# A two-block transformer on one core: joined attention streams, head norms beside a linear, additions on GpSimd and modulation slabs in unused halves of tiles

## The chip, the cores and the metric

One NeuronCore of one Trainium2 chip. The time is that of one launch of the kernel on the device, in microseconds (us). The profile is one execution of it. Engines: PE is TensorE, DVE is VectorE, ACT is ScalarE, POOL is GpSimd, SP is SyncE, which here only issues DMAs.

## The reference

256 latent tokens and 256 context tokens of width 1024 (fp32) go through two blocks of two layers each. Every layer is modulated by six vectors computed from `c` (for the latent) and `c_ctx` (for the context) by a 1024 x 6144 matrix.

```python
def first_block(...):                       # layers 0 (even) and 1 (odd)
    m_lat = split(silu(c) @ ada_w[l] + ada_b[l], 6); m_ctx = split(silu(c_ctx) @ ada_w[l] + ada_b[l], 6)
    h_lat, h_ctx = modulate(x_lat, m_lat[0], m_lat[1]), modulate(x_ctx, m_ctx[0], m_ctx[1])
    # even: 8 heads of global attention (2 kv heads, rms norm of q and k heads, rope), and
    #       8 heads of neighbourhood attention with a bias; odd: window attention with a sink, rope
    y_lat, y_ctx = even_mixer(...) or odd_mixer(...)
    x = layer_norm(DN_ALPHA * x + m[2] * y)
    x = layer_norm(DN_ALPHA * x + m[5] * conv_ffn(modulate(x, m[3], m[4])))

def token_mixer(...):                       # both layers of the second block
    y_a = conformer_conv(h)                 # glu, depthwise conv of 31 taps, norm, silu, projection
    y_b = diff_finish(softmax(q1 k1) v - lam * softmax(q2 k2) v)      # 8 heads of width 128, rope
    y_c = multiscale_pool(h)                # windows 2, 4, 8, 16, a small matrix per group
    g = sigmoid(h @ w_g + b_gate)
    return (g[..., :D] * y_a + g[..., D:2 * D] * y_b + g[..., 2 * D:] * y_c) @ w_out

def second_block(...):
    x = x + gt1 * rms_norm_2(token_mixer(rms_norm_2(x) * (1 + sc1) + sh1))
    x = x + gt2 * rms_norm_2(swiglu(rms_norm_2(x) * (1 + sc2) + sh2))
```

Layer 0 of a block computes latent and context (512 columns), layer 1 only the latent (256 columns), with the context entering its keys and values. The output is the latent after the second block.

## The kernel before

Activations lie with features on the 128 partitions, in chunks of 128 features: `X` (the residual), `O`, `SC`, `G` (32 chunks, named `big` in the trace), `QK` and others, each chunk 512 columns wide, latent left and context right. In layers 1 the right halves of most are unused.

Every linear is made of groups of one output chunk. A weight tile and an activation are each split into a high and a low part of the fast fp32 form, and a tile takes three matmuls (high·high L604, high·low L605, low·high L606), so 24 for a group of eight tiles. Weights come as slabs of 512 KB (one group) from DRAM: SP issues them in the order of `plan_linears` into a ring of four slots (L554), each waiting until the slab three before it is used up. ScalarE casts a slab to its high part (`w_high`, L1035), VectorE subtracts to get the low part (`w_low`, L1672); both work two slabs ahead of TensorE. On each engine the helper `turns` runs, for every group, first the cast or low of the slab two ahead, then the body of the group (bias, copy, residual and so on). So whatever stands in a body delays the next cast or low on that engine. Linears use banks 0 and 1 in turn.

The modulation vectors are linears of two rows: a part such as `1_0_2` (block 1, layer 0, third pair) is 16 slabs, whose products (L652) accumulate in a bank; ScalarE copies the rows (`mod_copy`, L1088), TensorE turns them to columns (`mod_turn`, L678), VectorE adds the bias and stores them (`mod_store`, L1689). Parts run beside the attention units (`BESIDE`, `mods_until`), or from eleven further slots, `spare_slabs` (`plan_spare` says behind which group's slab SP issues each, L559; `SPARE_ORDER` gives the slot), with the products put beside or between the statistics before up1_0, up2_0 and up2_1.

`attend` runs a list of units (a pair of heads by a tile of queries). TensorE makes scores two units ahead (L756), VectorE takes maxima (L1917), ScalarE the exps (L1321), TensorE turns the probabilities (L766) and multiplies by values (L779, L781). Block 1 layer 0 has two lists one after the other, `global` and `near`, layer 1 `window`; the second block's are `diff_0` and `diff_1`. At the end of the first three TensorE waits for the rows of the parts beside, turns them, and waits for their store before the next linear. `begin` makes the first two casts and lows of the linear that follows.

Block 1, layer 0 starts with `ev_qk` (13 groups: chunks 0 to 4 of `G` are the queries and keys that want a head norm) and `ev_v`. The head norms stand in the bodies of ev_v: square (ScalarE, already in ev_qk), head sum (TensorE), root (ScalarE, L1380), reciprocal and scale (VectorE, L2017, L2018), then the rope (TensorE L716, VectorE L1891 to 1893).

`mix1_1`, the output linear of layer 1's attention, has in the bodies of VectorE the scalings of the second block's context (`ctx_normed`, L1840), ready for `k_0_ctx` that follows; GpSimd sums the rows of x (L2360, L2363). od_q to od_k, and k_0_ctx to up1_1, are seams: statistics, norm and modulation of the next input spread over the eight groups of one linear.

In the second block p, q, k, v and gate linears carry the taps of the depthwise conv on VectorE (L2185, `TAP_SHARE` taps per group). After the three gate linears and the small `group_l` come diff_l, `branch_l` (16 groups of four tiles; VectorE multiplies each with its gate, L2239, and for every second one adds, L2244), `merge_l` (the attention branch, multiplied and added the same way, then cast by ScalarE, L1609), `out_l` with squares and their sums (GpSimd, L2374), and `up2_l`.

The lines that decide the order of weights and slots:

```python
for parts, places in ((("1_1_0",), [("mix1_0", g, 3) for g in (4, 5, 6)] + [("mix1_0", 7, 2), ("up1_0", 3, 5)]),
                      (("2_1_0", "2_1_1"), [("merge_0", g, 1) for g in (5, 6, 7)] +
                       [("out_0", g, 2) for g in (4, 5, 6, 7)] + [("up2_0", 3, 21)]),
                      (("2_1_2",), [("merge_1", g, 1) for g in (5, 6, 7)] +
                       [("out_1", g, 2) for g in (4, 5, 6, 7)] + [("up2_1", 3, 5)])):
```

## Time and profile before

| | |
|---|---|
| three runs | 2701.58, 2695.85, 2697.10 us, median 2697.1 |
| the profiled execution | 2698.55 us, its span 2696.7 us |
| granted TensorE clock, mean over the span | 0.983 |
| TensorE busy | 2554.9 us, 95% |
| VectorE, ScalarE, GpSimd busy | 1621.5, 1272.9, 210.5 us |
| DMA | 393.64 MB, mean 146 GB/s |
| chain that ended last | TensorE 82%, VectorE 8%, ScalarE 4%, DMA 3% |

The matmuls fill most of the span, so the rest of the time lies in many short waits of TensorE. The columns of the windows below are, for each stretch, its length and the busy time of each engine, then the granted clock (PEclk, 1.00 is full speed), the busy share of the 16 DMA engines, and what they moved. A timeline row has in brackets how long the engine had been idle before it and whose work ended that.

### The profile page before, as it was taken

What the parts mean: (1) busy time and instruction counts of PE and PEld (TensorE: products, weight loads), DVE (VectorE), ACT (ScalarE), POOL (GpSimd) and SP (SyncE); (2) the same over time, 40 slices, a digit from 0 to 9 for tenths busy, and PEclk for the clock granted to TensorE, in tenths of its full rate; (3) what the DMA queues carried; (4) which work ended last, traced back from release to release, by engine and by line L of the source; (5) the groups of instructions that cost most, each with busy time, mean ns of one, the idle gap of its engine ahead of it and who ended that gap; (6) DMA issues with size and microseconds to landing.
All of it is one profiled execution on the core that took longest, in us unless ns stands there. A gap on an engine that the chain in (4) does not pass through costs nothing.

```text
span 2696.7 us, 43197 instructions
## 1 busy us (share of the span) xinstructions
PE 2554.9 (95%) x16774; PEld 2153.5 (80%) x16774; DVE 1621.5 (60%) x2654; ACT 1272.9 (47%) x2372; POOL 210.5 (8%) x218
## 2 busy tenths in 40 slices
PE   7999999999988999999999999999999999987997
PEld 4855678889856999988886687688889999686997
DVE  2476466553687786668756763533326798665554
ACT  3355363433666665633336733422225645754443
POOL 3000100001201000324000001000001130001000
PEclk9999999999999999999999999999999999998999
DMA  7237422224554455534324435423235555145554
GB/s 274 93 126 265 188 85 95 95 92 135 164 186 162 156 185 170 174 102 144 115 89 145 149 125 182 185 94 100 84 113 156 177 175 167 64 137 192 182 174 143
DMA packets 119418, 393.64 MB, mean 146 GB/s; under 512 B 13728, under 2 KB 15776, under 8 KB 119136
## 3 DMA queue, kind: packets, MB, share of 16 engines
q1 hardware_dynamic: 117392, 386.47, 43.9%
q0 software_dynamic: 1872, 5.02, 0.7%
q8 instruction: 108, 1.77, 0.3%
q14 instruction: 46, 0.38, 0.1%
HBM read 390.39 MB, written 1.05 MB: 145 GB/s over the span
## 4 chain that ended last, share of the span: by engine, by line
PE 82%; DVE 8%; ACT 4%; DMA 3%; issue 1%; POOL 1%; SPq 0%; ACTq 0%; DVEq 0%; POOLq 0%
PE bank L604 24%; PE bank L605 23%; PE bank L606 23%; PE bank L756 2%; PE bank L652 2%; PE bank L766 2%; DVE w_low L1672 2%; PE bank L781 1%; DVE smax L1917 1%; PE bank L686 1%; ACT w_high L1035 1%; DVE conv_space L2185 1%; DMA spare_slabs<-in_w_mod 1%; PE bank L779 1%; PE bank L716 1%
## 5 line engine op out<-in xcount | busy, mean ns | idle before, releaser
L604 PE MATMUL bank<-h_high,w_high 128*128 128x256 f32 (+1 forms) x3168 | 1055.7, 333 | 52.3 <-DVE w_low L1672 14.1
L1672 DVE TENSOR_TENSOR w_low<-ring,w_high 128x1024 fp32r<-128x1024 f32 (+2 forms) x604 | 682.7, 1131 | 631.6 <-ACT w_high L1035 629.3
L606 PE MATMUL bank<-h_high,w_low 128*128 128x256 f32 (+1 forms) x3168 | 1039.2, 328 | 0.0
L605 PE MATMUL bank<-h_low,w_high 128*128 128x256 f32 (+1 forms) x3040 | 995.3, 327 | 0.0
L1035 ACT CAST w_high<-ring 128x1024 fp32r<-128x1024 f32 (+2 forms) x604 | 574.4, 953 | 293.7 <-DMA ring<-in_w_down 161.1
L604 PEld LDWEIGHTS bank<-h_high,w_high 128*128 128x128 f32 x3168 | 608.9, 192 | 113.6 <-issue 33.6
L606 PEld LDWEIGHTS bank<-h_high,w_low 128*128 128x128 f32 x3168 | 609.0, 192 | 50.6
L605 PEld LDWEIGHTS bank<-h_low,w_high 128*128 128x128 f32 x3040 | 584.2, 192 | 49.0 <-issue 0.7
L604 PE MATMUL bank<-f_high,w_high 128*128 128x256 f32 (+1 forms) x880 | 269.3, 306 | 2.4 <-DVE w_low L1672 2.3
L605 PE MATMUL bank<-f_low,w_high 128*128 128x256 f32 (+1 forms) x880 | 267.7, 304 | 0.0
L606 PE MATMUL bank<-f_high,w_low 128*128 128x256 f32 (+1 forms) x880 | 267.7, 304 | 0.0
L604 PEld LDWEIGHTS bank<-f_high,w_high 128*128 128x128 f32 x880 | 168.1, 191 | 10.7 <-DVE w_low L1672 3.4
L605 PEld LDWEIGHTS bank<-f_low,w_high 128*128 128x128 f32 x880 | 168.1, 191 | 7.0
L606 PEld LDWEIGHTS bank<-f_high,w_low 128*128 128x128 f32 x880 | 168.1, 191 | 6.8
L2185 DVE SCALAR_TENSOR_TENSOR conv_space<-big,vec,conv_space 128x512 f32<-128x512 f32 (+1 forms) x240 | 150.4, 672 | 1.3
L1321 ACT ACTIVATE h_space<-bank,smax 128x512 f32<-128x512 f32 (+1 forms) x192 | 116.3, 609 | 71.2 <-DVE smax L1917 70.5
L1444 ACT ACTIVATE conv_space<-bank,vec 128x512 f32<-128x512 f32 (+1 forms) x88 | 59.1, 672 | 178.2 <-PE bank L606 177.1
L1917 DVE TENSOR_REDUCE smax<-bank 128x1 f32<-128x512 f32 (+1 forms) x192 | 108.5, 597 | 35.3 <-PE bank L756 33.2
L2076 DVE SCALAR_TENSOR_TENSOR conv_space<-bank,vec,conv_space 128x510 f32<-128x510 f32 (+1 forms) x88 | 54.2, 616 | 100.6 <-ACT conv_space L1444 100.6
L604 PE MATMUL bank<-o_halves,w_high 128*128 128x512 f32 (+1 forms) x256 | 90.6, 354 | 12.0 <-DVE w_low L1672 5.5
L1639 ACT ACTIVATE conv_space<-bank 128x512 f32<-128x512 f32 (+1 forms) x44 | 21.6, 491 | 153.8 <-PE bank L606 153.8
L766 PEld LDWEIGHTS bank<-con,h_space 128*128 128x128 f32 x480 | 52.5, 144 | 49.6 <-issue 25.4
(232 smaller groups left out, 2664.2 us busy)
## 6 DMA issues: line engine op xcount, KB each, us to landing
ring<-in_w_up SPq DMA_DIRECT2D x176, 512.0 KB, 3.4
ring<-in_w_mod SPq DMA_DIRECT2D x112, 512.0 KB, 4.0
spare_slabs<-in_w_mod SPq DMA_DIRECT2D x64, 512.0 KB, 7.6
ring<-in_w_down SPq DMA_DIRECT2D x80, 384.0 KB, 3.1
ring<-in_w_down SPq DMA_DIRECT2D x80, 320.0 KB, 3.0
ring<-in_w_gate SPq DMA_DIRECT2D x48, 512.0 KB, 3.4
ring<-in_w_k SPq DMA_DIRECT2D x32, 512.0 KB, 3.5
ring<-in_w_v SPq DMA_DIRECT2D x32, 512.0 KB, 3.4
```

What stands on the lines that cost most here:

```text
L604: pe.matmul(out, wh[:, cols], high, start=first, stop=False)
L605: pe.matmul(out, wh[:, cols], low, start=False, stop=False)
L606: ins = pe.matmul(out, wl[:, cols], high, start=False, stop=last)
L652: ins = pe.matmul(bank[b][32 * q:32 * q + MOD_ROWS, 0:256], padded[:, first:first + MOD_ROWS], slab[:, 256 * q:256 * (q + 1)], start=(k == ...
L766: ins = pe.transpose(bank[5 + k % 2][:, t * P:(t + 1) * P], src[:, t * P:(t + 1) * P], IDENT)
L1035: nc.scalar.copy(wh[:, cols], raw[:, cols]).then_inc(high_ready, 1)
L1321: nc.scalar.activation(PROB[j % 6][:, 0:unit["T"]], banks[j % 4][:, 0:unit["T"]], ACT.Exp, bias=m, accum_out=ssum[:, j % NS:j % NS + 1]).t ...
L1444: nc.scalar.activation(SC[:, at.u, 0:w], bank[at.u % 2][:, 0:w], ACT.Identity, scale=vcol(l, at.g + (V1["conv_w"] + 2 * FC)), bias=vcol(l, ...
L1672: v.tensor_tensor(wl[:, cols], raw[:, cols], wh[:, cols].bitcast(F32), ALU.subtract).then_inc(low_ready, 1)
L1917: ins = v.reduce_max(m, sc[:, 0:w], AX_X, negate=True)
L2076: v.scalar_tensor_tensor(y[:, :, 1:S], u[:, :, 0:S - 1], vcol(l, at.g + V1["conv_w"]), y[:, :, 1:S], ALU.mult, ALU.add).then_inc(tap_left, 1)
L2185: ins = v.scalar_tensor_tensor(cvs(c), U[:, c, 0:ns, k:k + S], vcol(l, V2["conv_w"] + c * CONV_TAPS + k), cvs(c), ALU.mult, ALU.add)
```

## The change

1. `global` and `near` become one list `block1` of 32 units. Its three parts of modulation run two slabs per unit in the first 16 units and one after. Only the first part is turned ahead of the mixing linear, the others beside its group 2, and their stores stand in VectorE's bodies of groups 3 and 4 (layer 0) or 7 (layer 1); in layer 1 the order of the two parts changes. The parts' columns lie in banks of their own.
2. Head norms go from ev_v's bodies to those of ev_qk: squares in groups 1 to 5, roots and reciprocals in 3 to 7, ropes in 8 to 12.
3. merge_0 and merge_1 use banks 4 and 5.
4. GpSimd makes the eight context scalings in mix1_1, and in layer 1 of block 2 all 16 additions of branch and merge.
5. The 16 slabs of part `2_1_2` go to unused right halves of `G`, `QK`, `X`, `O` and `SC` (pieces of 1 KB per partition and quarter), 14 of them issued behind slab 3 of branch_1, two behind slab 3 of up2_1.
6. Of part `2_1_1`, slabs 0 and 1 stand beside the squares' statistics, ten before up2_0 and four beside its group 3; copy, turn and store come after up2_0.
7. In the two seams VectorE modulates chunks 2, 5 and 7, and ScalarE spreads its part over groups 4, 5 and 6.
8. The first casts and lows of branch_l start at unit 30 of diff_0 (31 before) and at unit 2 of diff_1 (before: VectorE ahead of it, ScalarE in group_1); branch_l waits for its inputs chunk by chunk.
9. Two conv taps per group in p_0, four before.

```diff
-            "global": units_pair(0, 4, 0, 0, range(4), None, False, True),
-            "near": units_pair(5, 9, 4, P, range(4), lambda h, qt: BIAS[:, h, qt, :], False, False),
+            "block1": units_pair(0, 4, 0, 0, range(4), None, False, True) +
+                      units_pair(5, 9, 4, P, range(4), lambda h, qt: BIAS[:, h, qt, :], False, False),
...
+            if slabs == 48:
+                return min(2 * u, 16 + u)
...
+        self.bank = 4 if name.startswith("merge") else 0
...
-                    out = bank[at.u % 2][:, 0:L.n]
+                    out = bank[L.bank + at.u % 2][:, 0:L.n]
...
-                          (("2_1_2",), [("merge_1", g, 1) for g in (5, 6, 7)] +
-                           [("out_1", g, 2) for g in (4, 5, 6, 7)] + [("up2_1", 3, 5)])):
+                          (SPARE, WIDE, 0, ("2_1_2",), [("branch_1", 3, WIDE), ("up2_1", 3, 2)])):
...
+        SPARES += [t[:, 4 * i:4 * i + 4, S:TOK] for t, count in ((G, 6), (QK, 2), (X, 2), (O, 2), (SC, 2)) for i in range(count)]
...
-        TAP_SHARE = [{"glu": 6, "p": 4, "q": 2, "kv": 0, "gate": 5}, {"glu": 4, "p": 2, "q": 3, "kv": 1, "gate": 4}]
+        TAP_SHARE = [{"glu": 6, "p": 2, "q": 2, "kv": 0, "gate": 5}, {"glu": 4, "p": 2, "q": 3, "kv": 1, "gate": 4}]
...
-                if not diff:
-                    pe.wait_ge(rows_copied, n["rows"] + len(beside))
-                    for part in beside:
-                        mod_turn(part)
-                        stored()
...
+                parts = BESIDE[("block1", "window")[l]]
+                pe.wait_ge(rows_copied, n["rows"] + len(parts))
+                mod_turn(parts[0])
+
+                def turns_beside(g):
+
+                    if g == 2:
+                        for part in parts[1:]:
+                            mod_turn(part)
...
-                linear(f"branch_{l}", branch_halves, [(h_ready, halves - 4)], extra=head)
+                linear(f"branch_{l}", branch_halves, extra=head)
...
-                    if l == 0 and c < 6:
-                        spare_slabs("2_1_0" if c == 0 else "2_1_1", (15,) if c == 0 else (c - 1,))
+                    if l == 0 and c in (0, 2, 4):
+                        spare_slabs("2_1_0" if c == 0 else "2_1_1", (15,) if c == 0 else (c // 2 - 1,))
...
-                        dve.wait_ge(ctx_in, 16)
-                        inverse(S, first=S)
-                    if 1 <= g < 5:
-                        for c in range(2 * g - 2, 2 * g):
-                            scaled(c, 1)
+                        n["root"] += 1
+                        n["stat"] += 1
+                        dve.wait_ge(root_ready, n["root"])
+                        v.reciprocal(RS_[:, S:TOK], RS_[:, S:TOK]).then_inc(ctx_inverse, 1)
...
-                    if space == c:
+                    if space == c or l == 1:
                         return
...
+                    pool.wait_ge(ctx_inverse, 1)
+                    for c in range(KC):
+                        g.tensor_tensor(O[:, c, S:TOK], X[:, c, S:TOK], RS_[:, S:TOK], ALU.mult).then_inc(t_ready, 1)
...
+                if l == 1:
+                    branch, merge = (LIN[f"{k}_1"].empty0["vector"] for k in ("branch", "merge"))
+                    for c in range(KC):
+                        pool.wait_ge(emptied["vector"], branch + 2 * c + 2)
+                        m = G[:, c, 0:S]
+                        g.tensor_tensor(m, m, G[:, 16 + c, 0:S], ALU.add).then_inc(merge_step, 1)
+                    pool.wait_ge(merge_step, 24)
+                    for c in range(KC):
+                        pool.wait_ge(emptied["vector"], merge + c + 1)
+                        m = G[:, c, 0:S]
+                        g.tensor_tensor(m, m, G[:, 8 + c, 0:S], ALU.add).then_inc(merge_step, 1)
```

VectorE at the end of ev_qk and in ev_v, before (`w_low` is the low part of a slab; `big<-big` of 128x512 twice is the bias plus mask of the near attention):

```order
L1672 TENSOR_TENSOR w_low<-ring,w_high 128x1024 x14
L2012 TENSOR_TENSOR big<-big 128x512 x2
L2017 RECIPROCAL rstd<-rstd 128x512
L2018 SCALAR_TENSOR_TENSOR big<-big,small,rstd 128x512
L1672 TENSOR_TENSOR w_low<-ring,w_high 128x1024
L2012 TENSOR_TENSOR big<-big 128x512 x2
L2017 RECIPROCAL rstd<-rstd 128x512
```

and now, from group 2 of ev_qk on:

```order
L1710 TENSOR_TENSOR w_low<-ring,w_high 128x1024 x4
L2052 RECIPROCAL rstd<-rstd 128x512
L2053 SCALAR_TENSOR_TENSOR big<-big,small,rstd 128x512
L1710 TENSOR_TENSOR w_low<-ring,w_high 128x1024
L2052 RECIPROCAL rstd<-rstd 128x512
L2053 SCALAR_TENSOR_TENSOR big<-big,small,rstd 128x512
L1710 TENSOR_TENSOR w_low<-ring,w_high 128x1024
```

The reciprocals and scales stand between the lows of ev_qk, no longer behind all of them.

VectorE in mix1_1 before (`x<-x,tmp` is the residual of a group, `l_space<-x,rstd` the scaling of a context chunk):

```order
L1672 TENSOR_TENSOR w_low<-ring,w_high 128x1024
L1758 SCALAR_TENSOR_TENSOR x<-x,tmp 128x256
L1835 RECIPROCAL rstd<-rstd 128x256
L1672 TENSOR_TENSOR w_low<-ring,w_high 128x1024
L1758 SCALAR_TENSOR_TENSOR x<-x,tmp 128x256
L1840 TENSOR_TENSOR l_space<-x,rstd 128x256 x2
L1672 TENSOR_TENSOR w_low<-ring,w_high 128x1024
L1758 SCALAR_TENSOR_TENSOR x<-x,tmp 128x256
L1840 TENSOR_TENSOR l_space<-x,rstd 128x256 x2
```

and now:

```order
L1710 TENSOR_TENSOR w_low<-ring,w_high 128x1024
L1796 SCALAR_TENSOR_TENSOR x<-x,tmp 128x256
L2092 RECIPROCAL rstd<-rstd 128x256
L1710 TENSOR_TENSOR w_low<-ring,w_high 128x1024
L1796 SCALAR_TENSOR_TENSOR x<-x,tmp 128x256
L1710 TENSOR_TENSOR w_low<-ring,w_high 128x1024
L1796 SCALAR_TENSOR_TENSOR x<-x,tmp 128x256
```

The scalings are gone from VectorE; GpSimd has them behind its sums of squares of the context.

SP's queue in layer 1 of the second block, before:

```order
L554 DMA ring<-in_w_branch 128x512 x16
L554 DMA ring<-in_w_merge 128x1024 x6
L559 DMA spare_slabs<-in_w_mod_1_2 128x1024
L554 DMA ring<-in_w_merge 128x1024
...
L554 DMA ring<-in_w_out 128x1024
L559 DMA spare_slabs<-in_w_mod_1_2 128x1024 x2
L554 DMA ring<-in_w_up_1 128x1024 x4
L559 DMA spare_slabs<-in_w_mod_1_2 128x1024 x5
```

and now:

```order
L561 DMA ring<-in_w_branch 128x512 x4
L567 DMA big<-in_w_mod_1_2 128x4x256 x6
L567 DMA qk<-in_w_mod_1_2 128x4x256 x2
L567 DMA x<-in_w_mod_1_2 128x4x256 x2
L567 DMA l_space<-in_w_mod_1_2 128x4x256 x2
L567 DMA conv_space<-in_w_mod_1_2 128x4x256 x2
L561 DMA ring<-in_w_branch 128x512 x12
L561 DMA ring<-in_w_merge 128x1024 x8
L561 DMA ring<-in_w_out 128x1024 x8
L561 DMA ring<-in_w_up_1 128x1024 x4
L567 DMA big<-in_w_mod_1_2 128x4x256 x2
```

Fourteen slabs moved from between the merge and out weights to a place ahead of twelve branch weights.

## Rows read from the trace of the kernel before

**Rows 1.** The page: busy us, share of the span, instructions by engine.

```profile
PE 2554.9 (95%) x16774; PEld 2153.5 (80%) x16774; DVE 1621.5 (60%) x2654; ACT 1272.9 (47%) x2372; POOL 210.5 (8%) x218
```

**Rows 2.** Windows (stretches in us from the span's start), columns in the first row.

```profile
core 0: us, PE busy (x) PEld busy (x) DVE busy (x) ACT busy (x) POOL busy (x), PEclk, DMA share, GB/s
116.00:144.00 28.00, 28.00 (x124) 21.86 (x123) 24.88 (x24) 9.69 (x14) 0.00 (x0) 1.00 0.23 75
144.00:164.00 20.00, 13.97 (x75) 7.30 (x75) 13.40 (x27) 10.32 (x25) 0.00 (x0) 0.74 0.19 59
203.00:216.00 13.00, 9.78 (x76) 5.43 (x76) 8.50 (x22) 6.02 (x17) 0.00 (x0) 0.87 0.43 142
217.00:261.00 44.00, 42.86 (x479) 24.23 (x477) 31.80 (x88) 28.00 (x80) 0.00 (x0) 1.00 0.86 293
831.00:872.00 41.00, 31.08 (x226) 28.84 (x223) 27.05 (x50) 23.22 (x40) 4.77 (x6) 0.92 0.33 110
1219.00:1245.00 26.00, 20.20 (x151) 19.34 (x150) 26.00 (x22) 8.34 (x13) 23.03 (x19) 0.93 0.40 128
1680.00:1709.00 29.00, 24.15 (x244) 6.89 (x240) 22.20 (x33) 11.05 (x21) 0.00 (x0) 0.94 0.94 370
2324.00:2374.00 50.00, 42.99 (x256) 27.55 (x256) 42.71 (x101) 39.89 (x117) 0.00 (x0) 0.97 0.04 16
2406.00:2439.00 33.00, 26.53 (x193) 25.16 (x194) 19.39 (x35) 10.53 (x15) 0.00 (x0) 0.93 0.51 181
2439.00:2469.00 30.00, 26.47 (x196) 25.61 (x200) 8.74 (x10) 11.63 (x23) 5.81 (x5) 0.91 0.68 263
```

**Rows 3.** Timeline: start, us, engine, line, out<-in; idle before <-releaser. Ropes.

```profile
146.23 3.35 DVE L2017 RECIPROCAL rstd<-rstd 128x512 f32<-128x512 f32 x1 [1.77 <-ACT rstd L1380]
...
150.43 1.05 PE L716 MATMUL bank<-big,con 128*128 128x256 f32 x2 [4.08 <-DVE big L2018]
```

**Rows 4.** Timeline: TensorE at the second stream's start and before mix1_0.

```profile
210.73 0.49 PE L756 MATMUL bank<-big 64*128 64x256 f32 x2 [2.36 <-ACT h_space L1321]
...
270.29 1.03 PE L678 MATMUL bank<-pick,conv_space 128*128 128x16 f32 x4 [2.27 <-DVE mod L1689]
```

**Rows 5.** Timeline of mix1_1: VectorE, GpSimd, TensorE.

```profile
848.89 1.30 DVE L1840 TENSOR_TENSOR l_space<-x,rstd 128x256 f32<-128x256 f32 x2
849.06 0.85 POOL L2360 TENSOR_TENSOR h_space<-x 128x256 f32<-128x256 f32 x1 [19.20 <-DVE x L1758]
...
853.17 0.36 PE L604 MATMUL bank<-o_halves,w_high 128*128 128x256 f32 x1 [1.28 <-DVE w_low L1672]
```

**Rows 6.** Groups by line and form: xcount, busy us, mean ns of one, idle before.

```profile
L1672 DVE TENSOR_TENSOR w_low<-ring,w_high 128x1024 fp32r<-128x1024 f32 x412 | 516.2, 1254 | 428.0 <-ACT w_high L1035 426.4
...
L2185 DVE SCALAR_TENSOR_TENSOR conv_space<-big,vec,conv_space 128x512 f32<-128x512 f32 x120 | 93.6, 829 | 0.8
...
L2244 DVE TENSOR_TENSOR big<-big 128x256 f32<-128x256 f32 x16 | 6.8, 425 | 0.5
...
L2374 POOL TENSOR_TENSOR qk<-qk 128x256 f32<-128x256 f32 x6 | 7.0, 1162 | 278.5 <-ACT qk L1190 278.5
```

**Rows 7.** Timeline: TensorE at branch_0.

```profile
1533.06 0.77 PE L604 MATMUL bank<-h_high,w_high 128*128 128x512 f32 x1 [3.38 <-issue]
```

**Rows 8.** Timeline of layer 1 of block 2: diff_1, merge_1, up2_1.

```profile
2326.54 0.70 PE L756 MATMUL bank<-qk 64*128 64x512 f32 x2 [2.97 <-ACT conv_space L1560]
...
2406.88 0.55 PE L604 MATMUL bank<-o_halves,w_high 128*128 128x256 f32 x1 [3.60 <-DVE big L2239]
...
2418.39 0.41 ACT L1609 CAST h_high<-big 128x256 fp32r<-128x256 f32 x1 [2.08 <-DVE big L2244]
...
2481.19 0.37 ACT L1088 COPY conv_space<-bank 128x256 f32<-128x256 f32 x1 [2.22 <-PE bank L652]
```

**Rows 9.** DMA issues: xcount, KB each, median us from issue to landing.

```profile
spare_slabs<-in_w_mod SPq DMA_DIRECT2D x64, 512.0 KB, 7.6
...
x<-in_ctx POOLq DMA_DIRECT2D x1, 1024.0 KB, 5.9
```

More of the change, by code:

```diff
@@ L1347, in attend @@
                         finish(c)
-                if beside:
+                if beside and not diff:
                     mod_copy(beside[-1])
@@ L1963, in attend @@
                         finish(c)
-                    if opens is not None and units[u]["diff"] and u == len(units) - 1:
-                        begin(LIN[opens], ahead)
+                    if u == BRANCH_FROM.get(name):
+                        begin(LIN["branch" + name[4:]], ahead)
                 store(len(units) - 1)
@@ L1968, in attend @@
                 n["unit"] += len(units)
[L1969 removed]
+                if opens is not None:
                     begin(LIN[opens], ahead)
[L1971 to L1973 removed]
                 dve.wait_ge(o_ready, n["unit"])
```

249 lines of the change are left out of this document (141 added, 108 removed).

## The prediction

> **What bounds the kernel now.** I read the page's busy times first: TensorE is busy for 2554.9 of 2696.7 us, VectorE for 60%, ScalarE for 47% [rows 1]. What an edit off TensorE can win lies in 142 us of TensorE idle, and in stretches where the granted clock is below 1.00. Then I took TensorE's idle times one by one from the timeline and made a table of the stretches that the change touches [rows 2]. In it the reader should look at three columns: the idle time (length less PE busy), PEclk, which falls behind long gaps (0.74 in the stretch 144 to 164, 1.00 in the one before), and DMA share. Last I read, row by row, who ends each gap [rows 3 to 8].
>
> **The sum, part by part.** Each term is against the profiled execution, 2698.55 us (span 2696.7). The median of the runs shown is 2697.1, 1.5 below; its scatter makes 0.2% (5.4 us) about what a measurement tells from no change.
>
> *Head norms beside the query linear.* Now they run in ev_v, and the rope at 150.43 waits 4.08 us for VectorE's scale, itself behind a 3.35 us reciprocal [rows 3]. TensorE idles 6.0 of the 20 us and the clock is 0.74, a loss of up to 5.2 us, of which I give 3 to busy time [rows 2]. Moved into ev_qk groups 3 to 7, each group gives VectorE 3.35 of reciprocal, about 0.8 of scaling and a weight low of 1.25 [rows 6]: 5.4 in all. A group's 24 matmuls of 512 columns take 5.4 by the 124 in 28 us of 116 to 144 [rows 2], and a head sum comes on top. It just fits. About 1.1 us of value copies and the first maxima stay. 6.0 + 3 − 1.1 gives 7.9; I take **−7**, range −9 to −4.
>
> *One stream for two attentions.* In 203 to 216 TensorE idles 3.2 us and the clock is 0.87, 1.7 us [rows 2]; one gap, 2.36, waits for the first exps of the second stream [rows 4]. With the units running on, that goes, some 4.9 us with the clock. One more wait for a copy of rows and the busier first half give back about 2 (my estimate, below the 2.36 above): **−3**, 0 to −5.
>
> *The modulation columns turned beside the mixing linear.* Before mix1_0 TensorE waits 2.27 us for VectorE's store between turns [rows 4]; now only one part is turned ahead. What is late next is VectorE's weight low, which ends just before: **−2.5**. At mix1_1 the same wait stands ahead of the linear; I take 2.7 there, with the turn itself.
>
> *Mixing linear of layer 1.* From 831 to 872 TensorE idles 9.9 us at clock 0.92 [rows 2]; gaps such as 1.28 at 853.17 wait for a weight low that waits behind the context's scalings [rows 5]. The change gives those eight to GpSimd. Of the gaps behind the start I take 5.5 back, leaving the rest to GpSimd's reads beside VectorE: with the start **−8.2**, −11 to −6. Against it speaks this: VectorE's two scalings at 848.89 took 1.30 us together while GpSimd's addition of 0.85 ran [rows 5]; two such instructions alone are 0.85, by the 425 ns of the same shape [rows 6]. The Trainium skill, "SBUF — State Buffer", section "Who interferes with whom", says that a VectorE instruction with two SBUF inputs and a GpSimd instruction that reads SBUF contend for a shared port, and that the one that comes first holds it until it ends. The row agrees: the two lost 0.45, part of one GpSimd instruction. By the rule alone the eight scalings would hold VectorE up by as much as 8 × 0.85, and the 5.5 would be gone; without contention nearly all 7.2 us behind the start would be had.
>
> *Conv taps.* p_0 has two taps per group fewer; VectorE is busy all 26 us from 1219 to 1245 and TensorE idles 5.8 of them, clock 0.93 [rows 2]. Two taps in each of four groups are eight instructions of 829 ns [rows 6], 6.6 us, moved behind this stretch into gate groups with room (the taps of all groups now come to 122, and 120 are needed): **−6**, −7 to −3.
>
> *Branch weights begin earlier.* branch_0 starts after a gap of 3.38 [rows 7], since VectorE's lows of the weights stood behind its lows of the chunks. The casts now start two units earlier, and the linear waits chunk by chunk. ScalarE's casts are late next: **−2.7**. In layer 1 diff_1 opens 2.97 late behind group_1's copies [rows 8]; that goes, but casts and lows of branch weights go into a loop where VectorE is busy 42.7 of 50 us [rows 2], which I price at half: **−1.4** with a small gain at branch_1's start; bounds −3 and +2.
>
> *Ten slabs before up2_0 instead of eleven, three beside the squares instead of six.* In 1680 to 1709 the DMA is at share 0.94 and TensorE idles 4.8 us [rows 2]: the slabs pace it. Four of them go behind three groups of up2_0: 4 × 0.5 gives **−2**.
>
> *Banks of their own.* merge_1 waits 3.60 us for a bank that the last branch product empties [rows 8]. A new bank frees the first matmul, but its weights and inputs are ready scarcely earlier: **−1** there, **−1** at out_0.
>
> *Merge additions on GpSimd.* In merge_1 a group is a ring: product and addition on VectorE, then ScalarE's cast, which waits 2.08 us for the addition [rows 8], then its weight cast, then the weight low. VectorE's addition is 0.42 [rows 6]. On GpSimd it costs 0.85 [rows 5], or 1.16 where it meets VectorE [rows 6], so +0.43 to +0.74, and I take 0.6 for seven groups: **+4.2**. Bounds 0 (the cast's delay is hidden behind TensorE) and +6. Beside the branch linear the eight additions are hidden: TensorE is waited for there.
>
> *Slabs in right halves.* Before, the spare loads stand between the slabs of merge_1 and out_1 in SP's queue, and from 2439 to 2469 TensorE idles 3.5 us at clock 0.91 [rows 2]. All fourteen now load during diff_1, where the DMA share is 0.04: **−3.9** with a little clock. ScalarE's copy of the rows at 2481.19 waits for the last product, and the root behind it [rows 8]; now only two slabs are late, or none: **−2.4**. No load of a slab costs TensorE anything; their products are the same number.
>
> *Seams.* VectorE makes three of eight modulated chunks: **−1**, 0 to −3, as the ScalarE chain before each is the longer one.
>
> Sum: −7 −3 −2.5 −8.2 −6 −2.7 −1.4 −2 −2 +4.2 −3.9 −2.4 −1 = **−37.9**, so 2660.6 for the profiled execution; with the median's 1.5 less that is 2659, and I say **2661** since the terms lean to the good side.
>
> **Rivals.**
> 1. *What is late next takes much of it.* Head norms at −4, taps at −3, the joined stream at 0, mix1_0's start at −1, diff_1 at +2: 3 + 3 + 3 + 1.5 + 3.4 is 14, so about 2675. For it: VectorE is the next limit in all five, and is busy 31.8 of 44 us in 217 to 261 already [rows 2]. Against it: the terms lie in separate stages and would all have to fail. Chance 0.14.
> 2. *VectorE and GpSimd hold each other up.* mix1_1 loses the 5.5; in merge_1 an addition that meets the 1.25 us weight low [rows 6] waits it out, 1.6 a group instead of 0.6: +7. Together 12.5: 2673. For it the 1.30 at 848.89 [rows 5] and the 1162 ns of a squares' addition on GpSimd [rows 6]; against it, VectorE is idle for 13.6 of the 33 us in merge_1 [rows 2]. This is the skill's rule above at full price. Chance 0.11.
> 3. *The clock never falls.* Length times (1 − PEclk) is 20 us over the eight touched stretches from 144 on [rows 2], part of it in idle time; some 8 are in my terms. If the gaps go whole, up to 12 more comes back: 2649. Chance 0.15.
> 4. *Slower: the right-half slabs block SP's queue.* They are issued behind the fourth branch slab and ahead of the other twelve, in pieces of 1 KB. If one takes t, branch_1 waits by 14t − 50 us, the 50 being diff_1. To undo the gain and more, 14t − 50 must pass 38: t over 6.3 us; at 7.6, the spare slabs' median from issue to landing [rows 9], it gives 56 us, 18 slower: 2716. But that median is of bursts of several; in 1680 to 1709 they moved at 370 GB/s, 1.4 us each, and the context's 1024 KB, also in 1 KB pieces, took 5.9, so 2.95 for such a slab [rows 9]: 41 us, which fits. Chance 0.03.
> 5. *The first units starve.* Two slabs per unit double the demand in the first half of the stream, and in the second stream as it is, with two per unit, the share is 0.86 at 293 GB/s [rows 2]. Burst traffic at 370 says there is room, yet landings may pace the units: +5, about 2666. Chance 0.04.
> 6. *It does not do what it says*: scaled chunks late for k_0_ctx, the reordering only moves waits, and nothing is gained: 2692 to 2697. Chance 0.03.
>
> **How the numbers follow.** My forecast has the rest, 0.50, for 2654 to 2668. The range takes in cases 1, 2, 3 and 5: 2646 to 2681, leaving out cases 4 and 6 and the outer tails of the others, about 0.16. Faster by over 0.2% (below 2691.7): all but case 4 and case 6: 0.94. Within: 0.03. Slower (above 2702.5): 0.03.
>
> **What would show it.** In the new profile: no TensorE gap over 1.5 us before the first scores, PEclk near 1.00 in that stretch, and VectorE's reciprocals inside ev_qk with TensorE unbroken; no gap at 204 to 211 but a DMA share over 0.9 early in the stream; mix1_1's eight groups in less than 27 us, with GpSimd scalings of 0.85 to 1.2; TensorE at 25 of 26 us in p_0 and q_0; merge_1 longer by 2 to 6 us with ScalarE's cast waiting for GpSimd; out_1 without waits for a weight's DMA; right-half slabs landing before 2374 of the old time. I am wrong if ev_qk grows by more than ev_v shrinks, if branch_1 waits for its slabs, or if GpSimd's instructions take over 1.5 us with VectorE's beside them as long.

## The result, and the profile after

The changed kernel takes 2666.2 us (median of four runs, 2663.8 to 2667.3) against 2697.4 before (four runs, 2695.9 to 2701.6): ratio 0.9881, interval 0.9864 to 0.9898. It is 31 us faster. That is 5 us above the forecast of 2661 and inside the range. The span of the profiled execution fell from 2696.7 to 2664.0 us, 32.7 us, and the mean granted clock rose from 0.983 to 0.987.

The page of the changed kernel, span and busy time by engine (the answer to [rows 1]):

```profile
span 2664.0 us, 43208 instructions
...
PE 2538.2 (95%) x16774; PEld 2145.0 (81%) x16774; DVE 1616.4 (61%) x2636; ACT 1270.8 (48%) x2366; POOL 229.7 (9%) x242
```

TensorE's busy time fell by 16.7 us although its instructions are the same 16774. I put that down to the clock: the stretches at half clock between 60 and 2640 us of the span fell from 82 to 48 us in total, and 34 us less of them can give back up to 17. The other 16.0 us are idle time of TensorE, 141.8 us before and 125.8 now.

Windows of the changed kernel around the work of [rows 2]. They don't all have the same length as there, so idle times are compared between the same matmuls in the table further down. Columns: length, busy us and instructions of PE, PEld, DVE, ACT, POOL, then PEclk, DMA share, GB/s.

```profile
144.00:158.00 14.00, 11.59 (x107) 6.22 (x110) 7.17 (x19) 9.81 (x24) 0.00 (x0) 1.00 0.48 176
193.00:206.00 13.00, 13.00 (x150) 7.33 (x144) 8.94 (x26) 7.47 (x21) 0.00 (x0) 1.00 0.85 309
822.00:853.00 31.00, 26.17 (x211) 25.08 (x207) 24.28 (x33) 20.75 (x38) 13.62 (x14) 1.00 0.39 126
1193.00:1225.00 32.00, 29.91 (x221) 28.96 (x220) 29.53 (x26) 12.59 (x18) 28.41 (x25) 0.95 0.46 146
1654.00:1680.00 26.00, 21.18 (x217) 7.72 (x210) 21.53 (x32) 10.35 (x19) 0.00 (x0) 1.00 1.02 404
2293.00:2344.00 51.00, 44.08 (x265) 28.19 (x265) 42.41 (x100) 41.20 (x121) 0.00 (x0) 1.00 0.51 166
2376.00:2409.00 33.00, 26.29 (x192) 24.90 (x192) 14.48 (x23) 9.28 (x14) 6.54 (x8) 0.95 0.37 127
2409.00:2437.00 28.00, 24.84 (x192) 24.64 (x192) 12.10 (x12) 13.95 (x25) 6.17 (x7) 0.94 0.45 144
```

What to see: the start of the first attention (144 to 158) idles 2.4 us at clock 1.00, where it idled 6.0 at 0.74. The joined stream (193 to 206) has no idle time at all. mix1_1 (822 to 853) idles 4.8 instead of 9.9, with GpSimd busy for 13.6 us in it. At 1193 to 1225 VectorE is no longer busy throughout. In diff_1 (2293 to 2344) the DMA share is 0.51 where it was 0.04. Before up2_0 (1654 to 1680) TensorE is as idle as it was, 4.8 us. merge_1 (2376 to 2409) is as idle as before.

Where the 32.7 us come from, by the first matmul of each linear in the two profiled executions. The measured column is the difference of the two intervals, the next one the part of it that is TensorE's idle time; much of the rest is clock:

| from, to | before, us | after, us | measured | of it idle | terms of the prediction |
|---|---|---|---|---|---|
| ev_qk, first scores | 116.9 | 111.0 | −5.9 | −4.9 | head norms −7 |
| first scores, mix1_0 | 119.0 | 112.3 | −6.7 | −0.3 | one stream −3, turns −2.5, and clock |
| mix1_0, up1_0 | 65.8 | 67.1 | +1.3 | 0.0 | not in the sum |
| od_q, mix1_1 | 127.3 | 125.8 | −1.5 | −1.0 | start −2.7, half of the seams |
| mix1_1, k_0_ctx | 33.6 | 27.8 | −5.8 | −3.3 | −5.5 |
| k_0_ctx, up1_1 | 29.7 | 28.7 | −1.0 | −1.0 | the other half of −1 |
| q_0, k_0 | 31.2 | 27.1 | −4.2 | −3.7 | taps −6 |
| k_0, branch_0 | 285.4 | 285.0 | −0.4 | −1.9 | branch weights −2.7 |
| branch_0, k_1_ctx | 547.9 | 545.4 | −2.5 | +0.2 | −1 and −2 |
| k_1_ctx, merge_1 | 325.9 | 323.1 | −2.8 | −0.3 | −1.4, and 0.9 by clock |
| merge_1, out_1 | 31.9 | 34.8 | +2.9 | +2.9 | +4.2 −1 |
| out_1, up2_1 | 49.6 | 43.9 | −5.8 | −3.9 | −3.9 −2.4 |

The second row deserves a look. TensorE's idle time there is 8.4 us before and 8.1 now. What fell is the time at half clock, from 13.2 to 0.9 us, and 8.0 of the 13.2 belong to one fall of 10.2 us that began at 150.6, in the gaps of the ropes and first scores.

The rest is within half a microsecond a stage. Timeline rows of the changed kernel, TensorE and ScalarE (start, us, then in brackets the idle time before and who ended it), for the places of [rows 3 to 5] and [rows 7, 8]:

```profile
150.17 0.70 PE L764 MATMUL bank<-big 64*128 64x256 f32 x4 [1.50 <-ACT h_space L1354]
...
182.64 0.62 PE L659 MATMUL bank<-ring,cvec_padded 128*8 128x256 f32 x8 [0.62 <-DMA ring<-in_w_mod]
...
258.93 0.77 PE L611 MATMUL bank<-o_halves,w_high 128*128 128x512 f32 x1 [2.31 <-DVE w_low L1710]
...
825.21 0.36 PE L611 MATMUL bank<-o_halves,w_high 128*128 128x256 f32 x1 [1.44 <-DVE w_low L1710]
...
839.33 0.35 PE L611 MATMUL bank<-o_halves,w_high 128*128 128x256 f32 x1 [1.48 <-DVE w_low L1710]
...
881.71 0.35 PE L611 MATMUL bank<-h_high,w_high 128*128 128x256 f32 x1 [3.68 <-DVE w_low L1710]
...
1216.16 0.36 PE L611 MATMUL bank<-h_high,w_high 128*128 128x256 f32 x1 [2.09 <-DVE w_low L1710]
...
1508.45 0.47 PE L611 MATMUL bank<-h_high,w_high 128*128 128x512 f32 x1 [1.26 <-DVE conv_low L1756]
...
2448.43 0.37 ACT L1112 COPY conv_space<-bank 128x256 f32<-128x256 f32 x1 [1.61 <-PE bank L659]
```

mix1_0 starts behind a gap of 2.31, and mix1_1 behind one of 1.44, that a weight low ends. Inside mix1_1 gaps of 1.48 and 0.89 are left. branch_0 still starts behind 1.26. ScalarE's copy of rows before up2_1 waits 1.61 for the last product, where it waited 2.22 [rows 8].

### The profile page after: what moved, and what is told of

Same layout as the page of the kernel before. It is cut to its first block, busy times and chain, and to the rows that moved or that the text cites. A ratio compares the mean times of both kernels' runs of the same rounds, so it can differ in the third digit from the quotient of the medians.

```text
span 2664.0 us, 43208 instructions
## 1 busy us (share of the span) xinstructions
PE 2538.2 (95%) x16774; PEld 2145.0 (81%) x16774; DVE 1616.4 (61%) x2636; ACT 1270.8 (48%) x2366; POOL 229.7 (9%) x242
## 4 chain that ended last, share of the span: by engine, by line
PE 83%; DVE 9%; ACT 4%; DMA 2%; issue 1%; POOL 1%; SPq 0%; ACTq 0%; DVEq 0%; POOLq 0%
PE bank L611 24%; PE bank L613 24%; PE bank L612 24%; PE bank L764 2%; PE bank L659 2%; DVE w_low L1710 2%; PE bank L774 2%; DVE smax L1962 1%; PE bank L789 1%; PE bank L694 1%; ACT w_high L1059 1%; PE bank L787 1%; DVE rstd L1880 1%; PE bank L724 1%; DMA first_slabs<-in_w_mod 1%
## 5 line engine op out<-in xcount | busy, mean ns | idle before, releaser
L613 PEld LDWEIGHTS bank<-h_high,w_low 128*128 128x128 f32 x3168 | 607.7, 192 | 50.7
L612 PEld LDWEIGHTS bank<-h_low,w_high 128*128 128x128 f32 x3040 | 583.5, 192 | 49.6 <-issue 1.7
L611 PE MATMUL bank<-o_halves,w_high 128*128 128x512 f32 (+1 forms) x256 | 89.6, 350 | 13.6 <-DVE w_low L1710 8.1
```

The source lines that it names most:

```text
L611: pe.matmul(out, wh[:, cols], high, start=first, stop=False)
L612: pe.matmul(out, wh[:, cols], low, start=False, stop=False)
L613: ins = pe.matmul(out, wl[:, cols], high, start=False, stop=last)
```

## The experiments

All start from the changed kernel unless the text says otherwise; times are medians, ratios are against the kernel before on the same chip. A difference of 2 or 3 us lies inside the intervals (the kernel before has medians of 2696.5, 2698.4 and 2699.4 beside these runs), so the verdicts on small terms rest on the profiles. There an untouched stage mostly repeats within a few tenths, with two exceptions. First, the granted clock falls to half at some long gaps in one execution and not in another, for 3.4, 6.8 or 13.7 us. od_q, which most of these edits leave alone, lasted 25.0 us with no time at half clock, 26.5 with 3.4 us of it, and 27.6 in the changed kernel's profile with 5.8. Below, "at equal clock" means that half of the time at half clock is taken off both. Second, two stages scatter for a reason that I don't know: ev_qk takes 79.6 to 81.1 us in the twelve profiles that leave it alone, with the same 0.29 us of idle time, and from the first scores to mix1_0 it is 111.3 to 112.5 us in ten that leave that part alone, partly because a wait of 0.6 us for a modulation slab at 182.6 is there or not.

### The additions of merge_1

merge_adds_vector:

```diff
-                    if space == c or l == 1:
+                    if space == c or l == 1 and space >= 16:
...
-                    pool.wait_ge(merge_step, 24)
-                    for c in range(KC):
-                        pool.wait_ge(emptied["vector"], merge + c + 1)
-                        m = G[:, c, 0:S]
-                        g.tensor_tensor(m, m, G[:, 8 + c, 0:S], ALU.add).then_inc(merge_step, 1)
```

> The changed kernel (2666.2 us) with the eight additions of merge_1 back on VectorE; the eight of branch_1 stay on GpSimd. My theory, that merge_1 is a ring through the addition: a group steps in 3.44 us in place of 3.90 in the changed kernel's profile, merge_1 is 3.2 us shorter, time 2663. Rival, that GpSimd's addition is hidden and the slower step comes from the banks or from less overlap: the step stays 3.90 and the time 2666.

Measured: 2665.5 us, ratio 0.9883 (0.9864 to 0.9901); span 2660.5 against 2664.0. The waits of TensorE in 33 us from merge_1's start, first of the changed kernel, then of this one (us in total, times, longest):

```profile
PE bank L611 <- DVE big L2289: 4.0, 6, 0.8
PE bank L611 <- DVE w_low L1710: 2.9, 1, 2.9
```

```profile
PE bank L611 <- DVE w_low L1710: 6.5, 2, 3.6
PE bank L611 <- DVE big L2289: 1.7, 6, 0.3
```

Six gaps of 0.8 became six of 0.3, and a group steps in 3.44 instead of 3.90; merge_1 to out_1 took 31.6 us instead of 34.8. The theory's 3.2 us are there in the profile; in the medians they do not show above the scatter. Of the change's 2.9 us here, 2.3 are five groups with 0.46 each, and the gap before out_1 grew from 3.90 to 4.52.

all_adds_vector takes the other eight additions back too (the whole GpSimd block goes, and the condition is `if space == c:`).

> All 16 additions of layer 1's merge back on VectorE. If GpSimd's eight additions beside branch_1 are hidden and VectorE's would be too, branch_1 is as long as in the changed kernel within 0.3 us and the time is that of merge_adds_vector, 2663. Rival, that branch_1 is bound by VectorE (it stepped better with the additions gone): branch_1 longer by up to 8 x 0.4 = 3 us, time 2666.

Measured: 2660.3 us, ratio 0.9863 (0.9845 to 0.9881), span 2657.9. branch_1 lasts 30.0 us against 29.7: the additions beside branch_1 are hidden on either engine, as expected. The time is 3 us under the expectation and 5 us under merge_adds_vector. The profiles are 2.6 us apart, and 2.1 of these lie at merge_1's start, where TensorE waited 2.2 in place of 2.9 and the clock fell for 0.4 us in place of 3.6. The rest of the 5 us is not explained.

### The slabs in right halves

spare_slots is all_adds_vector with the third line of `plan_spare` as before. It is built on that kernel because GpSimd's additions read the chunks over which the old slots lie.

> As all_adds_vector, and the 16 slabs of the last modulation part in their old slots and places in SP's queue. My theory, that the loads in the queue made out_1 wait and that the last slabs made the root late: from the first matmul of out_1 to that of up2_1 49.6 us as before the change, against 43.9: 5.8 us slower than all_adds_vector, 2669. Rival, that the right halves only moved the waits: under 2 us slower. In diff_1, TensorE's gaps stay as they are if DMAs do not disturb it.

Measured: 2668.5 us, ratio 0.9894 (0.9875 to 0.9913), 8.2 above all_adds_vector. From out_1's first matmul to up2_1's the profile has 48.6 us against 43.7. ScalarE's timeline in its out_1, each weight cast waiting for its slab:

```profile
2421.70 1.05 ACT L1060 CAST w_high<-ring 128x1024 fp32r<-128x1024 f32 x1 [2.23 <-DMA ring<-in_w_out]
...
2425.54 1.05 ACT L1060 CAST w_high<-ring 128x1024 fp32r<-128x1024 f32 x1 [2.23 <-DMA ring<-in_w_out]
...
2429.38 1.05 ACT L1060 CAST w_high<-ring 128x1024 fp32r<-128x1024 f32 x1 [2.23 <-DMA ring<-in_w_out]
...
2434.37 1.05 ACT L1060 CAST w_high<-ring 128x1024 fp32r<-128x1024 f32 x1 [3.39 <-DMA ring<-in_w_up]
```

So the loads between the weights in SP's queue did cost 5 us: out_1 lasts 2.7 us longer, and 2.2 more pass between its last matmul and up2_1. And the fourteen slabs in 1 KB pieces were no burden where they went: from group_1's first matmul to branch_1's it is 50.7 us with 6.7 us of TensorE idle time in both kernels, with the slabs' loads there and without them. DMA issues of the changed kernel in the stretch 2285 to 2360 (KB each, median us from issue to landing), with the GB/s of each of 40 slices above:

```profile
GB/s 6 30 35 0 35 208 303 208 288 360 364 348 348 349 352 341 347 349 273 49 0 0 0 0 4 0 9 0 0 0 0 0 14 126 140 9 164 127 189 151
...
ring<-in_w_branch SPq DMA_DIRECT2D x12, 256.0 KB, 2.7
big<-in_w_mod SPq DMA_DIRECT2D x6, 512.0 KB, 9.3
```

They move at some 350 GB/s, 1.5 us a slab, and are through in about 21 us. A single one takes 9.3 us to land because several are under way at once: the 7.6 us of [rows 9] was of that kind, and was no price per slab.

### The scalings of the context

scalings_vector:

```diff
+                        dve.wait_ge(ctx_in, 16)
+                        inverse(S, first=S)
+                    if 1 <= g < 5:
+                        for c in range(2 * g - 2, 2 * g):
+                            scaled(c, 1)
...
-                    pool.wait_ge(ctx_inverse, 1)
-                    for c in range(KC):
-                        g.tensor_tensor(O[:, c, S:TOK], X[:, c, S:TOK], RS_[:, S:TOK], ALU.mult).then_inc(t_ready, 1)
```

> The changed kernel with the eight scalings of the context back on VectorE. My theory, that GpSimd's help was worth the 5.6 us by which mix1_1 is shorter: its eight groups take about 32 us in place of 27.0, time 2671 to 2672. Rival, that the port that the two share eats the gain and that the rest came from the store of columns moved away: under 2 us longer, 2667.

Measured: 2673.6 us, ratio 0.9909 (0.9885 to 0.9934). mix1_1 took 34.4 us against 27.0 (34.2 against 27.8 to k_0_ctx's first matmul), and the gaps are those of before:

```profile
821.50:856.50 35.00, 27.94 (x198) 27.02 (x199) 23.21 (x39) 18.13 (x34) 4.78 (x6) 0.90 0.34 106
```

```profile
837.56 0.35 PE L611 MATMUL bank<-o_halves,w_high 128*128 128x256 f32 x1 [1.28 <-DVE w_low L1710]
...
841.94 0.36 PE L611 MATMUL bank<-o_halves,w_high 128*128 128x256 f32 x1 [1.29 <-DVE w_low L1710]
```

Of these 6.4 us to k_0_ctx, 3.1 are waits and 3.2 are clock (6.5 us at half clock against none). One fall of 3.4 us came at mix1_1's start, where all_adds_vector and branch_waits_four have it too, which leave mix1_1 alone; there it takes 29.3 us. So GpSimd's help is worth some 5 us here, 3.1 of them waits, about as much as the slabs; the median's 7 us hold falls of the clock in other stages too. Yet the two engines slow each other. VectorE and GpSimd of the changed kernel in mix1_1 (start, us, engine, line):

```profile
834.47 0.95 DVE L1796 SCALAR_TENSOR_TENSOR x<-x,tmp 128x256 f32<-128x256 f32 x1
837.62 1.56 DVE L1710 TENSOR_TENSOR w_low<-ring,w_high 128x1024 fp32r<-128x1024 f32 x1 [2.20 <-ACT w_high L1059]
839.11 0.95 DVE L1796 SCALAR_TENSOR_TENSOR x<-x,tmp 128x256 f32<-128x256 f32 x1
839.98 1.76 DVE L1710 TENSOR_TENSOR w_low<-ring,w_high 128x1024 fp32r<-128x1024 f32 x1
841.66 0.96 DVE L1796 SCALAR_TENSOR_TENSOR x<-x,tmp 128x256 f32<-128x256 f32 x1
```

```profile
833.55 8.79 POOL L2488 TENSOR_TENSOR l_space<-x,rstd 128x256 f32<-128x256 f32 x8 [14.09 <-DVE rstd L2092]
```

Eight scalings take 8.79 us, 1.1 each. Three of them fall into VectorE's idle 2.20 us and take 0.73 each; the three longest, beside VectorE's instructions, take 1.58 to 1.73. Beside them VectorE's residual is 0.95 in place of 0.42, and a weight low up to 1.76 in place of 1.22. Over the seven instructions from 833.4 to 843.5 VectorE loses 3.0 us, almost the 3.4 that the eight scalings cost it before. What was won is not VectorE's time: it is that scalings no longer stand between one group's residual and the next weight low in every group. The loss shows in the gap of 1.48 at 839.33, and perhaps in the one of 0.89 at 846.21. That the order is what was won is my reading of the steps; no run has the scalings on VectorE in another place.

### The head norms

norms_in_ev_v puts squares, head sums, roots, reciprocals, scales and ropes back where they were (all three engines' `head_norm`), with everything else changed.

> The changed kernel (2666.2 us) with the head norms and ropes back in ev_v; everything else stays. My theory: the gaps of 4.08 and 1.36 at the first attention's start return with their low clock, and ev_qk loses the 4.8 us by which its groups 3 to 12 are longer in the changed kernel; from the first matmul of ev_qk to the first scores 116.9 us as before the change, against 111.0: 5.9 us slower, 2672. Rival, that the norms are only moved and their TensorE time in ev_qk eats the gain: under 2 us slower.

Measured: 2672.6 us, ratio 0.9907 (0.9891 to 0.9924), 6.3 above the changed kernel (7 by the ratios). The gaps return:

```profile
149.16 1.22 PE L724 MATMUL bank<-big,con 128*128 128x256 f32 x2 [4.09 <-DVE big L2056]
151.78 3.57 PE L764 MATMUL bank<-big 64*128 64x512 f32 x8 [1.40 <-DVE big L1934]
156.19 0.70 PE L764 MATMUL bank<-big 64*128 64x256 f32 x4 [0.84 <-ACT h_space L1352]
```

From ev_qk's first matmul to the first scores 116.1 us against 111.0, and mix1_0 starts 5.5 later. In the changed kernel ev_qk's groups 3 to 7 step in 6.32 us and 8 to 12 in 5.89, where they all stepped in 5.44: TensorE's own head sums and ropes moved in, and the changed kernel's ev_qk lasts 6.4 us longer than this one's, and 5.5 longer than before the change. In return it has 11.5 us less from ev_v's first matmul to the first scores, 4.6 of them idle time.

### One stream, and the turns

two_streams has the old two lists with one and two slabs per unit; only the wait for copied rows is written for both.

> The changed kernel with the two attentions of block 1 as two streams, one modulation slab per unit in the first and two in the second, as before; the turns beside the mixing linear stay. My theory: the gaps of 0.48, 0.35 and 2.36 at the seam return, with 1.7 us of lost clock: 3 to 4 us slower, 2670. Rival, that the wait for the slabs and rows in the joined stream costs as much: same time.

Measured: 2668.0 us, ratio 0.9889 (0.9873 to 0.9906). The gap is back:

```profile
200.52 0.70 PE L764 MATMUL bank<-big 64*128 64x256 f32 x4 [2.33 <-ACT h_space L1356]
```

But from the first scores to mix1_0's first matmul it is 113.3 us against 112.3, and 0.9 to 2.0 above the ten profiles with this part untouched. With the joined stream TensorE waits three times for 0.57 us in the second half (at 221, 233 and 246) and has more slabs in the first, so that much of the 2.8 us of the seam's gaps is paid elsewhere. The clock did not fall at this gap here; before the change it did, for 3.4 us at 212. Of my term of −3, 1 to 2 us are waits, and 1.7 more come when the clock falls there.

turns_ahead puts all turns and stores ahead of the mixing linears:

```diff
-                mod_turn(parts[0])
+                for part in parts:
+                    mod_turn(part)
+                for part in parts:
+                    stored()
```

> The changed kernel with all turns of the modulation rows ahead of mix1_0 and mix1_1 and all stores ahead of the residuals. My theory: each linear starts later by the other turns and the wait for the last store, mix1_0 by 2.0 us, mix1_1 by 1.0, but the turns' TensorE time (1.3 us, in mix1_0's duration of 48.1 against 46.8) comes out of the linears: net 1.5 us slower, 2668. Rival, that the whole 2.5 and 2.7 us of the prediction hang on it: 5 us slower, 2671.

Measured: 2668.3 us, ratio 0.9889 (0.9873 to 0.9906). mix1_0 starts 5.4 us behind the attention's last matmul where it was 2.9, and lasts 1.6 less, 0.9 at equal clock. mix1_1 starts 4.1 us behind the attention instead of 2.9, behind a gap of 2.25 instead of 1.44. The net is about 1.5 us in layer 0 and 1 in layer 1, not the 2.5 and 2.7 of the prediction.

```profile
262.02 0.77 PE L611 MATMUL bank<-o_halves,w_high 128*128 128x512 f32 x1 [3.96 <-DVE mod L1719]
```

### The seams

seams_scalar is `BY_VECTOR = ()`.

> The changed kernel with all modulated chunks of the two seams on ScalarE (still over groups 4, 5 and 6). My theory: the gap before up1_1, 3.68 in the changed kernel and 4.71 before, is ScalarE's chain; it grows to 4.5 or more, 1 us slower, 2667, and the gaps around od_k (0.50 and 1.42) change by under 1 us. Rival, that VectorE's share only delays its weight lows: 1 us faster, 2665.

Measured: 2667.4 us, ratio 0.9886 (0.9870 to 0.9903). The gap before up1_1 is 4.40, against 3.68 in the changed kernel:

```profile
881.83 0.55 PE L611 MATMUL bank<-h_high,w_high 128*128 128x256 f32 x1 [4.40 <-DVE w_low L1710]
```

It grew by 0.7 us; I had expected 4.5 or more. k_0_ctx is 0.4 longer, but so it is in three profiles that leave the seam alone. The gap before od_k grew by 0.4, within what I expected.

### The taps

taps_four is `"p": 4` in layer 0.

> The changed kernel with four conv taps per group in p_0, as before. My theory, that the eight taps delay the weight lows of p_0 and q_0: q_0 lasts 31.4 us in place of 27.2, 4 us slower, 2670. Rival, that only the gap of 2.09 at q_0's start (still there with two taps) counts: under 1 us.

Measured: 2669.2 us, ratio 0.9891 (0.9866 to 0.9916). Window and gaps of its q_0:

```profile
1194.50:1226.50 32.00, 24.91 (x198) 23.94 (x198) 32.00 (x29) 11.16 (x17) 26.01 (x21) 1.00 0.41 132
```

```profile
1199.11 0.36 PE L611 MATMUL bank<-h_high,w_high 128*128 128x256 f32 x1 [1.07 <-DVE w_low L1710]
...
1204.91 0.36 PE L611 MATMUL bank<-h_high,w_high 128*128 128x256 f32 x1 [2.69 <-DVE w_low L1710]
```

q_0 lasts 31.4 us against 27.2, the 4.2 of the table. In waits it is more, 7.1 us against 2.1: in the changed kernel's q_0 the clock fell for 3.4 us, here it did not. In two profiles of a q_0 as changed without that fall it lasts 25.7. What the prediction missed is that one gap stays: 2.09 us before q_0's seventh group in the changed kernel, beside GpSimd, which is busy 28.4 of 32 us there.

### The waits of branch_0

branch_waits_four gives branch_0 and branch_1 back the wait for four chunks ahead of the first matmul.

> The changed kernel with branch_0 and branch_1 waiting for four chunks before their first matmul, as before. My theory, that branch_0's second group (which reads chunks 4 to 7) is set by VectorE's eight lows in a row, so that the first group's earlier start wins almost nothing: the first matmul about 1.5 us later, but the gap of 1.12 before the second group shrinks and the time is under 0.5 us longer, 2666. Rival, that the waits by chunk carry the gain: 1.5 to 2 us slower, 2668.

Measured: 2668.1 us, ratio 0.9884 (0.9858 to 0.9909), span 2667.4.

```profile
1509.28 0.77 PE L611 MATMUL bank<-h_high,w_high 128*128 128x512 f32 x1 [3.02 <-issue]
```

The first matmul comes behind 3.02 us instead of 1.26, and the gap of 1.12 before the second group is gone. So the two gaps are one supply, VectorE's eight lows. VectorE of the changed kernel there:

```profile
1507.23 0.35 DVE L1992 TENSOR_SCALAR l_space<-bank,srec 128x128 f32<-128x128 f32 x1 [0.87 <-PE bank L787]
1507.62 4.91 DVE L1756 TENSOR_TENSOR conv_low<-conv_space,h_high 128x512 fp32r<-128x512 f32 x8
```

Eight lows of 0.6 us run from 1507.62 to 1512.53, and the second group, which reads chunks 4 to 7, starts with the last. Still the stretch from group_0 to merge_0 is longer, 147.1 us, against 144.7 in profiles where the clock fell for 3.4 us in branch_0. Here it fell for 6.8. That the longer gap brought the longer fall is not shown: turns_ahead, which leaves this part alone, fell for 6.8 us too, behind a gap of 1.26, and took 146.0. Against that profile the wait for four chunks costs 1.1 us, between my expectation of under 0.5 and the rival's 1.5 to 2.

### The cast one group later

The first experiments showed merge_1 to be a ring in which ScalarE's weight cast stands behind its cast of the merged chunk. cast_one_later breaks it there and leaves the additions on GpSimd:

```diff
-                def merged(at):
-                    act.wait_ge(merge_step, n["merge"] + 8 + at.g + 1)
-                    nc.scalar.copy(HH[:, at.g, 0:w], G[:, at.g, 0:w]).then_inc(hh_ready, 1)
+                def merged(g):
+                    act.wait_ge(merge_step, n["merge"] + 8 + g + 1)
+                    nc.scalar.copy(HH[:, g, 0:w], G[:, g, 0:w]).then_inc(hh_ready, 1)
 
-                products(f"merge_{l}", merged)
+                products(f"merge_{l}", lambda at: merged(at.g - 1) if at.g else None)
+                merged(7)
```

> The changed kernel with ScalarE's cast of merged chunk g put one group later, behind the weight cast that follows, in merge_0 and merge_1; the additions stay on GpSimd. My theory, that merge_1 is slow only because the weight cast stands behind the addition's cast in ScalarE's order: with the cast later GpSimd's slower addition is off the ring and the groups of merge_1 step in TensorE's own 2.9 us in place of 3.90, merge_1 about 5 us shorter, 2661. Rival, that GpSimd's additions and VectorE's instructions hold each other up whatever the order: the step stays over 3.6, time 2665.

Measured: 2652.6 us, ratio 0.9825 (0.9800 to 0.9850), 14 us under the changed kernel. Waits of TensorE in 33 us from merge_1's start, and the window of the same stretch:

```profile
PE bank L611 <- DVE w_low L1711: 2.8, 2, 2.4
PE bank L611 <- ACT qk L1214: 0.4, 1, 0.4
PE bank L611 <- DVE big L2290: 0.2, 1, 0.2
```

```profile
2378.00:2411.00 33.00, 31.00 (x251) 30.41 (x252) 20.09 (x29) 14.52 (x22) 8.13 (x9) 1.00 0.46 152
```

Groups step in 2.9 us, TensorE's own time. From merge_1's first matmul to out_1's it is 24.2 us where it was 34.8; the gap of 4.5 before out_1 is in this, and 0.4 is left of it. With out_1 the profile has 12.1 us less. merge_0, where the cast is later too, does not change (44.1 us). The clock stays at 1.00 from 2378 to 2442. GpSimd's additions still meet VectorE's (two of them took 2.28 us at 2385), and cost nothing.

vector_adds_cast_later has all additions on VectorE and the cast later.

> All additions on VectorE, as in all_adds_vector (2660.3), and the cast one group later. Theory: the step falls from 3.44 to 2.9 us, 3 us under all_adds_vector, 2657, the fastest of all. Rival, that another chain (VectorE's product, addition and two lows) binds at 3.4: same as all_adds_vector.

Measured: 2655.1 us, ratio 0.9835 (0.9814 to 0.9856), span 2651.2: 5 us under all_adds_vector, and not told apart from cast_one_later. The groups step in 2.9 to 3.1 us. Off the ring it does not matter which engine adds.

## Why the prediction was right, and where it was off

The direction, the place of nearly every part and the size hold: 31 us of the 36 forecast. The make-up of the sum does not. By my own account some 8 of the 37.9 us were clock, and so about 30 were waits. The two profiles show 16.0 us less idle time and 16.7 us less busy time, which I put down to the clock. The waits gave about half of what I forecast and the clock twice its share, and that the two errors nearly cancel is luck.

- **Head norms**: −7 forecast, −5.9 measured, 5 to 6 by the undone change. "It just fits" was right: no more idle time in ev_qk than before. The sum left out that TensorE's own head sums and ropes stretch ev_qk by 5.5 to 6.4 us, and that a second gap of 1.50 opens behind the first scores. It also counted 3 us of clock, while the fall at 150.6 cost about 4 us more behind the first scores, in the next row of the table.
- **One stream**: −3 forecast, 1 to 2 us by the undone change. I counted the gap that goes whole and guessed 2 back; more came back. TensorE's idle time between the first scores and mix1_0 is 8.4 us before and 8.1 after, for this term and the next together. The slabs moved forward cost nearly as much as the seam. My rival of starving first units came only as one wait of 0.62 us at 182.64 for a slab: the DMA share is 0.85 at 309 GB/s in 193 to 206 with TensorE never idle.
- **Turns**: −2.5 and −2.7 forecast. By the undone change they are worth about 1.5 and 1 us. The wait for the store goes, but mix1_0 then waits 2.31 us for a weight low, which I had taken to end in time, and the turns stay TensorE's work: mix1_0 is longer by 1 us at equal clock, which the sum did not hold.
- **mix1_1**: −5.5 for its body, −5.8 measured, but I meant 5.5 of waits. They fell by 3.3, and the rest is clock (5.4 us at half clock before, none now). So the term came out in part by luck. Rival 2, that VectorE and GpSimd hold each other up, is right in its mechanism here (VectorE lost 3.0 us), and may account for the 2.2 us of waits that I counted too much.
- **Taps**: −6, −4.2 measured, one gap of 2.09 stays. Without a fall of clock in q_0 it is −5.7.
- **Branch weights**: −2.7 at branch_0's start, −0.4 measured there, because the clock fell for 3.4 us at 1425, in diff_0, in this execution. In nine profiles where it did not, k_0 to branch_0 is 283.5 us, −1.9. "ScalarE's casts are late next" was wrong: VectorE's eight lows are. In layer 1 −1.4 forecast, −1.9 measured from group_1 to merge_1, but only 0.3 of it is idle time: the opening gap fell from 2.97 to 0.66, and new waits in diff_1 and branch_1 took nearly all of that.
- **Fewer slabs before up2_0 and the bank of out_0**: −3 forecast, −2.5 measured. merge_0 is 1.2 us shorter, and 1.1 of it is idle time, as forecast for the bank. The slab term's reason is not borne out: between out_0 and up2_0 TensorE's idle time stays at 5.3 us. That stretch lost 4.4 us and up2_0 gained 2.5, since the four slabs' products moved from one to the other, and the 3.4 us at half clock before up2_0 did not come this time. No run undoes this part.
- **merge_1**: +4.2 −1 forecast, +2.9 measured, by 0.46 a group (I took 0.6) in five groups where I counted seven, and 0.6 before out_1; the new bank's share is the start gap, 2.92 for 3.60. The ring is shown by four runs.
- **Right halves**: −6.3 forecast, −5.8 measured against before, 4.9 against spare_slots. There it divides nearly as forecast, 2.7 in out_1 (3.9 forecast) and 2.2 before up2_1 (2.4). The slower rival 4 had 1.5 us a slab against its point of 6.3.
- **The clock**: rival 3 gave up to 12 us more than the 8 in my terms, and about 9 of it came. Half-speed time between 60 and 2640 us of the span fell from 82 to 48 us. The larger gaps (before mix1_0, merge_1, out_1, up2_1) kept their falls. In the profiles of the twelve other kernels, which are variants of the changed one, it is 37 to 68 us, so part of the 34 can be chance.

## What to carry to other kernels

Where a linear steps slower than TensorE's own time, write down the ring of what each engine does between two groups, in its program order; whatever stands ahead of the next group's cast or load in that order is on the ring, and one instruction put a group later (cast_one_later) was worth more than any part of the change, 12 us in its stage and 14 by the medians. A helper engine's slower instruction costs nothing off such a ring and its full surplus on it. And work that is moved from before a linear to beside it keeps its TensorE time: only the waits go.

## What the runs showed that I had not expected

- A GpSimd scaling of 128x256 is 0.73 us while VectorE is idle and up to 1.73 beside its instructions; VectorE's residual beside it goes from 0.42 to 0.95 us. Even at this price moving eight instructions took 3.1 us of waits away, some 5 us with the clock.
- The same gap brings a fall to half clock of 3.4 us, 6.8 us or none in different executions. Before branch_0 there is none with the gap of 1.26 in the changed kernel, 3.4 us with the same gap in cast_one_later, and 6.8 us with it in turns_ahead. Such a fall of 3.4 us cost 1.5 us in diff_0, in q_0 and in mix1_1 alike.
- In q_0 a fall of clock cost nothing where VectorE, busy throughout, sets the pace. With four taps it takes 31.2 us with 3.4 us at half clock (before) and without any (taps_four). With two taps it is 27.1 with that fall and 25.6 without.
- Fourteen loads of 512 KB in 1 KB pieces ran at some 350 GB/s beside an attention whose TensorE idle time did not change (6.7 us with them and, in spare_slots, without them).
